# Last and first weight pieces by tile of rows, kept norms as two row operations, and new lane scripts in a whole-model fp32 kernel

## The reference

```
for i in range(4):
    x = x + 0.5 * swiglu(rmsnorm(x, ffn1_norm[i]), ffn1_w_gu[i], ffn1_w_down[i])
    h = rmsnorm(x, mix_norm[i])
    m = (gated_deltanet, stick_breaking, dsa_sparse, gated_deltanet)[i](h, ...)
    x = x + m
    x = x + 0.5 * swiglu(rmsnorm(x, ffn2_norm[i]), ffn2_w_gu[i], ffn2_w_down[i])
x = rmsnorm(x, final_norm)
for l in range(2):
    mix = mixer_sublayer(x, ...)      # GLA, gMLP and MoBA branches, gated, then w_out
    x = layer_norm(ALPHA * x + mix, ln1_g[l], ln1_b[l])
    ff = square(relu(x @ w_ff1[l])) @ w_ff2[l]
    x = layer_norm(ALPHA * x + ff, ln2_g[l], ln2_b[l])
```

## Time and profile before

| | |
|---|---|
| median of 3 runs | 3136.65 us (3131.71 to 3138.2) |
| the profiled execution: its time / its span | 3133.97 / 3132.2 us |
| busy: TensorE, VectorE, ScalarE, GpSimd | 2981.8, 1785.0, 1608.3, 138.6 us |
| mean DMA rate over the span | 164 GB/s |
| stages: a feed-forward stage (905 to 1096) | 191.0 us, TensorE busy 191.0 |
| gdn (208 to 396), mixer2 (2180 to 2455), dsa (1285 to 1393) | 188, 275, 108 us, TensorE busy 170.4, 257.5, 87.8 |

### The profile page before, as it was taken

One profiled execution on the slowest core, in us unless ns is written; L12 is line 12 of the kernel. 1 busy time (PEld: TensorE's weight loads), 2 busy tenths in 40 slices (PEclk: granted clock), 3 DMA queues, 4 the chain that ended last, 5 costly groups with the idle time before them and its releaser, 6 DMA issues.

```text
span 3132.2 us, 36486 instructions
## 1 busy us (share of the span) xinstructions
PE 2981.8 (95%) x15042; PEld 2523.4 (81%) x15042; DVE 1785.0 (57%) x2147; ACT 1608.3 (51%) x2048; POOL 138.6 (4%) x122
## 2 busy tenths in 40 slices
PE   8999899999999999989999998998999998999998
PEld 6888788888988888768888887887878787878786
DVE  5558455455565455565555585654655645655644
ACT  5447754444454354555444467644556553456552
POOL 0004200000000000000000033000000000000000
PEclk9999999999999999989999999999999999999999
DMA  6554155555545565425555541455545555545553
GB/s 220 179 181 141 43 162 188 179 184 182 167 148 184 179 188 181 167 81 184 186 181 188 169 138 65 148 183 178 168 139 177 167 183 179 161 135 179 170 177 132
DMA packets 372694, 512.12 MB, mean 164 GB/s; under 512 B 11409, under 2 KB 239889, under 8 KB 372529
## 3 DMA queue, kind: packets, MB, share of 16 engines
q1 hardware_dynamic: 372528, 509.80, 51.3%
HBM read 508.70 MB, written 1.05 MB: 163 GB/s over the span
## 4 chain that ended last, share of the span: by engine, by line
PE 82%; DVE 6%; ACT 6%; DMA 2%; issue 1%; POOL 1%; SPq 0%; POOLq 0%; DVEq 0%; ACTq 0%
PE ps L424 24%; PE ps L426 24%; PE ps L425 24%; PE ps L509 3%; PE ps L496 2%; DVE lo L549 2%; ACT hi L531 2%; PE ps L456 1%; DVE qkv L1365 1%; PE ps L457 1%; PE ps L458 1%; PE ps L480 1%; POOL junkp L1557 1%; DMA raw<-in_ffn_w_gu 1%; POOL goz L1560 0%
## 5 line engine op out<-in xcount | busy, mean ns | idle before, releaser
L549 DVE TENSOR_TENSOR lo<-raw,hi 128x2048 fp32r<-128x2048 f32 (+1 forms) x479 | 1072.3, 2244 | 929.9 <-ACT hi L531 929.4
L531 ACT ACTIVATE hi<-raw 128x2048 fp32r<-128x2048 f32 (+2 forms) x489 | 911.7, 1869 | 706.4 <-DMA raw<-in_ffn_w_gu 254.9
L424 PE MATMUL ps<-hi,xh 128*128 128x512 f32 (+1 forms) x2208 | 876.1, 397 | 8.7 <-DVE xl L624 4.1
L426 PE MATMUL ps<-hi,xl 128*128 128x512 f32 (+1 forms) x2208 | 861.4, 390 | 0.0
L425 PE MATMUL ps<-lo,xh 128*128 128x512 f32 (+1 forms) x2208 | 860.1, 390 | 0.0
L424 PEld LDWEIGHTS ps<-hi,xh 128*128 128x128 f32 x2208 | 416.5, 189 | 92.5 <-issue 6.8
L426 PEld LDWEIGHTS ps<-hi,xl 128*128 128x128 f32 x2208 | 415.8, 188 | 87.6
L425 PEld LDWEIGHTS ps<-lo,xh 128*128 128x128 f32 x2208 | 416.9, 189 | 81.0
L424 PE MATMUL ps<-hi,hh 128*128 128x512 f32 x704 | 276.1, 392 | 0.0
L426 PE MATMUL ps<-hi,hl 128*128 128x512 f32 x704 | 274.2, 390 | 0.0
L425 PE MATMUL ps<-lo,hh 128*128 128x512 f32 x704 | 274.0, 389 | 0.0
(11 more groups left out here) (438 smaller groups left out, 3254.6 us busy)
## 6 DMA issues: line engine op xcount, KB each, us to landing
raw<-in_ffn_w_gu SPq DMA_DIRECT2D x352, 512.0 KB, 4.8
raw<-in_ffn_w_down SPq DMA_DIRECT2D x80, 1024.0 KB, 5.1
raw<-in_w_ff SPq DMA_DIRECT2D x64, 1024.0 KB, 5.4
raw<-in_w_in SPq DMA_DIRECT2D x60, 1024.0 KB, 5.3
raw<-in_gdn_w_in SPq DMA_DIRECT2D x32, 1024.0 KB, 5.7
raw<-in_sb_w_in SPq DMA_DIRECT2D x12, 1024.0 KB, 5.2
raw<-in_w_branch SPq DMA_DIRECT2D x12, 1024.0 KB, 5.0
raw<-in_ffn_w_down SPq DMA_DIRECT2D x16, 512.0 KB, 3.5
```

Of the source, the lines that this page charges most:

```text
L424: e.matmul(o, a1, r1, start=kk == 0, stop=False)
L426: i = e.matmul(o, a2, r1, start=False, stop=kk == kts - 1)
L531: k.e.activation(k.m.hi[q % RING][:, 0:n], k.m.raw[q % RING][:, 0:n], ACT.Copy).then_inc(*k.up("act_piece_hi", ("hi", q)))
L549: k.e.tensor_tensor(m.lo[i][:, 0:n], m.raw[i][:, 0:n], m.hi[i][:, 0:n].bitcast(F32), ALU.subtract).then_inc(*k.up("dve_piece_lo", ("split" ...
```

## The change

In parts:

1. **Late pieces.** The last piece of a stage (`late` 1), or the last three where a kept norm follows (`late` 3), is run for tile 0 first and then for tile 1 (`tensor_piece` with `ts`; `tensor_out`). `vector_out` takes its residuals in that order.
2. **First pieces.** mixer2 starts with `mu` and `mz`, ff2 with its first two column groups, the first three pieces of which are run for tile 0 and then for tile 1 (`tensor_rows_two`); the stages that start with columns (gdn now with `k` instead of `ba`; sb) run the first halves of their first two pieces, then the second halves (`first=2`).
3. **Kept norms.** The statistics come from bn_stats for the rms norm too (mean and variance, then mean² + variance); each tile has its own root. x becomes (x - mean) * gain, then x * root + bias, both scalar_tensor_tensor over 128x512 (for the rms norm x * root * gain alone). x is turned per tile (`tensor_turn_kept`), `xh` and `xl` are plain copies and differences. `rows_gained` is gone, on GpSimd too. The norm is now a lane in the script, with `next` in all stages.
4. **Output** in two transfers, one a tile.
5. **Scripts** written out for all stages, gdn's new. Gelu, Silu and Sin of mixer2 have a step of their own, `gelu`. Some waits are added that the new orders need.

```diff
 class Plan:
     def out(self, W, kts):
         for s in range(2):
             self.rows(("dn", self.g, s), W, 512 * s, 512, kts)
+        self.late |= set(range(len(self.pieces) - self.lates[self.g], len(self.pieces)))
     def gdn(self, t, name, i):
+        self.cols(("k", g), W, 1024, 4)
         self.cols(("ba", g), W, 3984, 1)
-        self.cols(("k", g), W, 1024, 8)
+        self.cols(("k", g), W, 1024, 8, first=4)
...
+        self.late.add(self.of[("dn", g, 1)][-1][0])
     def mixer2(self, t, name, l):
+        for n, c0 in (("mu", 2064), ("mz", 2576)):
+            self.rows((n, g), W, c0, 512, 8)
...
     def steps(self, p):
-        if len(dims) == 2 and dims[0] == 8:
+        if len(dims) == 2 and dims[0] == 8 or p in self.late:
             return 2
...
+        self.late = 3 if after else 1
...
+def tensor_rows_two(k, plan, pids, xh, xl, ready):
+    banks = {pid: tensor_banks(k, pid, 512) for pid in pids}
+    pieces = [(pid, piece) for pid in pids for piece in plan.of[pid]]
+    for t in range(2):
+        for pid, piece in pieces[:3]:
+            yield from tensor_piece(k, plan, pid, piece, (t,), banks[pid], xh, xl, 8, 512, ready)
+    pid, piece = pieces[3]
+    yield from tensor_piece(k, plan, pid, piece, (0, 1), banks[pid], xh, xl, 8, 512, ready)
...
+def tensor_out(k, plan, si, h, l, kts, ready):
+    banks, pieces = {}, [(("dn", si.g, s), piece) for s in range(2) for piece in plan.of["dn", si.g, s]]
+    early = len(pieces) - si.late
+    for pid, piece in pieces[:early]:
...
+        yield from tensor_piece(k, plan, pid, piece, (0, 1), banks[pid], h, l, kts, 512, ready)
+    for t in range(2):
+        for pid, piece in pieces[early:]:
...
+            yield from tensor_piece(k, plan, pid, piece, (t,), banks[pid], h, l, kts, 512, ready)
+def tensor_turn_kept(k, g, t):
+    for s in range(2):
+        b = k.take("xT", g, t, s)
         k.wait_ge(*b.before)
+        k.wait_ge("x", g, t, s)
+        for j in range(4):
+            i = k.e.transpose(b.ps[:, j * P:(j + 1) * P], k.m.x[:, t, (4 * s + j) * P:(4 * s + j + 1) * P], k.m.C(C_ID))
...
 def vector_norm(k, si):
+    for t in range(2):
+        mean, var, rt = (st[:, c:c + 1] for c in (88 + 2 * t, 89 + 2 * t, 94 + t))
...
+        e.bn_aggr(st[:, 88 + 2 * t:90 + 2 * t], st[:, 64 + 12 * t:76 + 12 * t]).then_inc(*k.up("dve_bn", ("ms" if ln else "var", g, t)))
...
         if ln:
+            k.wait_ge("ms", g, t)
+            for s, (xs, gain, _) in enumerate(x):
+                e.scalar_tensor_tensor(xs, xs, mean, gain, ALU.subtract, ALU.mult).then_inc(*k.up("dve_x_normed", ("xc", g, t, s)))
+            k.wait_ge("rt", g, t)
+            for s, (xs, _, bias) in enumerate(x):
+                k.wait_ge("xc", g, t, s)
+                e.scalar_tensor_tensor(xs, xs, rt, bias, ALU.mult, ALU.add).then_inc(*k.up("dve_x_normed", ("x", g, t, s)))
...
+FFN_SCRIPT = """
+W x1 W W W gate W W W W W turn W gate W W gate gate W W W W turn W W W W W gate W W W W turn W W W gate W turn
+W gate W turn turn W gate turn gate W W W W W W W W W turn W W W turn W gate W gate W W W W W turn turn W out
+W W W W W W W W W W W W W next out out W W
+"""
...
 GDN_SCRIPT = """
+clear x1 rbc W c3 W c0 rbc W E ba W E W W gates gates E W gates W E c2 gates W W W nk gates gates W c2 c0 E W
+nk nk W c1 nk E nk kT c0 c2 W nk c0 c2 c1 c3 E W c1 c3 W c1 E W inv c3 E kT W E W W inv gates W W W W W W c0 W
+c3 c2 E c1 c0 W c2 E c0 nq W Z W c2 W nq nq c2 c0 W nq nq nq c0 c2 qk c1 c2 c3 sv c1 c3 W Z c0 c1 rows rows c1
+c0 c3 rows c1 c3 rows c2 c0 gate c1 c3 a0 qk c1 c2 a0 a0 a1 a0 c3 a0 qk qk a1 c3 a0 a0 a1 W a1 a1 a1 W W a1 W
+W out W W next out W out
 """
...
+SB_SCRIPT = """
+x1 W rbc W E W W W E rbc E W E W W W E W W heads W heads W heads W E heads W E heads E W heads W heads W W v W
...
+DSA_SCRIPT = """
+W x1 W W W p0 W normq normq W W W normq W p1 normk W normk W W normk normk W W qi index_q normk W uq turn_q
+index_q index turn_q W index index index uv index index index turn_q turn_q W index index W uk W turn_k
+attention attention attention attention attention attention attention attention attention W W attention
+attention attention out W W W W next out out W W
...
+MIXER2_SCRIPT = """
+W W x1 W mu W W angles mz W lr clear W angles W W W W W decays W W decays W decays gk decays W gq W decays W W
+decays decays gv gla W decays W W decays W W gla W gla W gg gla gla gla gelu gla gla gla W W W W gmlp gla gla
+gla gmlp gmlp gla gmlp gmlp gla gla moba gla oq W W ok gmlp W W gmlp W gla W gmlp W W moba ov gmlp gmlp moba W
...
+next out W norm W
+"""
...
     for r in range(2):
         for s in range(2):
-            k.wait_ge("xr", infos[-1].g, r, s)
-    e.dma_start(out[0].rearrange("(t p) d -> p t d", p=P), m.x[:, :, :]).then_inc(*k.up("dma_out", ("out",), by=16))
+            k.wait_ge("x", infos[-1].g, r, s)
+        e.dma_start(out[0, r * P:(r + 1) * P, :], m.x[:, r, :]).then_inc(*k.up("dma_out", ("out", r), by=16))
```

More of the change, by code:

```diff
@@ L241, in run, with __init__ @@
         assert name not in script or next(lane, "end") == "end", name
-def to_next(si):
-    return ["next"] if si.after is None and not si.last else []
 class Plan:
-    def __init__(self, t, stages):
-        self.pieces, self.of, self.stage, self.pool = [], {}, [], set()
+    def __init__(self, t, stages, lates):
+        self.pieces, self.of, self.stage, self.pool, self.late, self.lates = [], {}, [], set(), set(), lates
         for g, (name, *arg) in enumerate(stages):
@@ L403, in tensor_rows @@
     w = n // half
[L404 to L433, removed]
@@ L434, in tensor_rows @@
+    for t in ts:
         if k0 + cnt == kts:
-            for b in banks[0] + banks[1]:
+            for b in banks[t]:
                 k.close(b)
-        yield
[L440 to L446, removed]
-        k.wait_ge(*b.before)
[L448 to L461, removed]
-                k.close(b)
-            yield
@@ new lines, in tensor_rows_two, with tensor_cols @@
+def tensor_rows_two(k, plan, pids, xh, xl, ready):
[6 more added lines that the diff above has]
+    yield from tensor_piece(k, plan, pid, piece, (0, 1), banks[pid], xh, xl, 8, 512, ready)
+def tensor_cols(k, plan, pid, xh, xl, ready, first=0):
+    pieces = plan.of[pid]
+    steps = [tensor_col_piece(k, plan, pid, piece, xh, xl, ready) for piece in pieces]
+    for _ in range(2):
+        for step in steps[:first]:
+            next(step)
+            yield
+    for step in steps[first:]:
+        for _ in range(2):
+            next(step)
+            yield
@@ L945, in turn @@
             yield
[L947 to L948 removed]
+    run(script, {"W": vector_pieces(k, plan, g), "x1": vector_x1(k, si), "turn": turn(),
+                 "out": vector_out(k, si, 1.0, keep=ALPHA), "norm": vector_norm(k, si), "next": vector_next(k, nxt)})
 def gdn_room(m):
@@ L2690, in tensor_program @@
         TENSOR[si.name](k, plan, si, nxt, SCRIPT[si.name](plan, si))
-        if si.after and not si.last:
-            run(["x0"], {"x0": tensor_turn_x(k, nxt.g, 0)})
 def scalar_program(k, plan, infos):
@@ L2700, in scalar_program @@
         SCALAR[si.name](k, plan, si, nxt, SCRIPT[si.name](plan, si))
-        run(["norm"], {"norm": scalar_norm(k, si)})
-        if si.after and not si.last:
-            run(["x0"], {"x0": scalar_turned_x(k, nxt, 0)})
 def vector_program(k, plan, infos):
@@ L2711, in vector_program @@
         VECTOR[si.name](k, plan, si, nxt, SCRIPT[si.name](plan, si))
-        run(["norm"], {"norm": vector_norm(k, si)})
-        if si.after and not si.last:
-            run(["x0"], {"x0": vector_turned_x(k, nxt, 0)})
-        elif si.after:
-            vector_gained(k, nxt, 0)
-            vector_gained(k, nxt, 1)
 def pool_program(k, plan, infos):
-    for si, nxt in zip(infos, infos[1:] + [None]):
-        if si.before:
-            run(["rows", "rows"], {"rows": (step for s in range(2) for step in pool_gained(k, si, s))})
+    for si, nxt in zip(infos, infos[1:]):
         if si.name in POOL:
```

462 lines of the change are left out of this document (251 added, 211 removed).

## The result

The changed kernel takes **3034.68 us** (median of 4 runs, 3033.87 to 3036.35) where the kernel before took 3135.72 beside it (4 runs): ratio 0.968, 95% interval 0.9663 to 0.9696, 101 us faster.

A forecast was written before the change was run, and what follows sets the result against it. TensorE, busy 2981.8 of 3132.2 us, bounds the kernel; only its idle time and lower-clock stretches can be won. Terms 31 + 6 + 8 + 16 + 16 + 5 - 6 = 76 us gave 3061 us, range 3022 to 3108.

The forecast's parts named there:

- mixer2: Inner gap before the sum of gv's matmuls goes, no VectorE split before the sum, four W steps ahead: gain 16 us.
- gdn: Wait behind the convolution in both gdn stages falls from 11 to some 3 us: gain 16 us, or 0 if splits collide.
- likeliest case: The forecast's main case, all terms summed to 76 us gained: chance 0.59, own range 3040 to 3082 us.
- slower: Rival: feed-forward gates ahead of splits make 17 places cost about 5 us each, 3146 us; chance 0.09.
- Kept norms with late pieces: Four boundaries before and after mixer2 and ff2 lose 14 us instead of 44.7: gain 31 us, 22 to 35.
- The end: Behind the last matmul: 9.4 us from tile 1's end, 4.4 of it for the output to land; gain 6 us.
- Ordinary boundaries: Last piece by tiles shortens stage entries: two gdn entries 2.0 us each, sb 4; together 8 us.
- inner gaps stay: Rival: gaps inside gdn, mixer2 and dsa remain as chains keep their length, 3098 us; chance 0.17.
- dsa: Top-k mask steps come before three weight steps and two pieces run inside attention: gain 5 us, 0 to 10.
- Feed-forward scripts: Some 17 places in eight stages where the gate makes ScalarE and the next split wait: loss of 6 us.
- More is won: Rival: inner gaps go whole, lanes lose nothing, TensorE's busy time holds lower-clock work; 110 us gained, 3027; chance 0.11.

The follow-up runs named there:

- both_whole: Changed kernel with only the last piece by tiles at kept norms, turning of tile 0 behind the last matmuls, and mixer2's and ff2's first pieces for both tiles: 3075.19 us.
- late_one: Changed kernel with only the last weight piece, not three, tile by tile at the four kept norms, turning of tile 0 behind the last matmuls: 3058.63 us.
- parts: Changed kernel: second gdn without GpSimd splits, both mixer2 with two W steps ahead, second also a split ahead of the sum, output in one transfer: 3053.78 us.
- old_lanes: Changed kernel with the old interleaving in feed-forward stages, sb, dsa and gdn, and gdn's old piece order; tails, kept norms and mixer2 as changed: 3064.64 us.
- pool_sets: Changed kernel with one of gdn's five GpSimd splits given back to VectorE, the first in the first gdn, the second in the second: 3039.17 us.
- improved: Changed kernel with the norm's early table load behind the last Silu of the last feed-forward stage, and tile 0's turning one step later at three kept boundaries: 3028.33 us.

## Why the prediction was right or wrong

The direction and the mechanism of the kept norms and of mixer2 were right; gdn, of equal size in the forecast, failed. The sum was 25 us short (76 for 101): six terms gave more than forecast, together some 40 us, and gdn gave 16 less. So that the total fell into the range is in part luck, and it missed the likeliest case, 3040 to 3082. Two sums don't come out as written. The ends of the terms taken half together give 3049 to 3089 for that case; and the rival "slower" subtracts the 6 us of the gates from the gain and then counts its places in full, so its 3146 should be 3140.

- *Kept norms with late pieces*, 31 (22 to 35), measured 39 by both_whole. The waits came as the prediction had them: 8.5 in all where it had 2.5 a boundary, 1.4 to 1.9 at three of them and 3.4 at the first, for the table load that the working did not have. The step that was mis-sized is the lower clock: the 1.0 a boundary that I added for it was not paid in the changed kernel's trace, and what the old pauses cost does not end with the windows of the earlier trace rows. late_one measures such a price: 11 us more of waiting cost 21. That the gain is overlap and not the cheaper norm is shown by both_whole, for the four inner boundaries.
- *The end*, 6, measured 7.7. The chain of passes is as laid out (4.9 us from the last matmul's start to the issue); the transfer is the part mis-sized, 3.1 us for a last half where I took 4.4 for the whole. 1.4 of it is shown by the single transfer in parts.
- *Ordinary boundaries*, 8. gdn's entries gave 2.3 each for 2.0. sb gave 8.1 for 4: 4.3 of that with its interleaving, which the term had not counted, so the entry's share is 3.8. The sizes were right. Of the two reasons given for gdn, old_lanes shows that the split's place in VectorE's queue is needed; the last piece by tiles does nothing without it.
- *gdn*, 16 (0 to 22), measured near 0: the two stages are 4.2 us shorter, and their entries give 4.5. This is the step that failed, by the rival "inner gaps stay", which the page "SBUF — State Buffer" of the Trainium skill (section "SBUF: two separate sides") had spoken for with its exclusive lock; the trace agrees with it. A GpSimd split of 6.73 beside two of VectorE that take 8.88, and a second one with a convolution of 5.6 us under it, are the old collision at other steps (the convolution that held TensorE up before now takes 2.5); two waits at the head of the stage (1.4 and 2.7) are new. The waits of 0.4 us and more inside the first gdn add up to 16.0 us before and 16.5 after, and TensorE's work at the lower clock in the two gdn stages grew from 11.8 to 18.0 us. But the lock is half of it: without any GpSimd split the stage gets longer, since VectorE's queue then has a split ahead of the chain's copy.
- *mixer2*, 16 (4 to 18). With the kept norms it makes the last four stages and the ffn2 ahead of them 60.8 us shorter, for 31 + 16; 39 taken off, 22 are left for it. The trace of the kernel before holds as much inside mixer2: the two waits of 7.3, 8.3 us of work at the lower clock behind them (half of it lost), and smaller waits of 0.7 and 1.1 in each layer, 22.4 in all. The gap went as the step says, and having it back costs 13.0 in one layer, 5 more than the waits themselves. Of the two reasons given the first holds (no split of VectorE ahead of the sum), the second doesn't: two W steps instead of four cost 0.2.
- *dsa*, 5 (0 to 10), measured 13. Mis-sized: the wait for the mask fell from 8.9 to 1.8 where I held the keys' turning against it, and two stretches at the lower clock in the old attention (PEclk 0.83 over 21 us in old_lanes, 1.00 now) went with it. Cover inside attention is 4 of it; the rest has no run of its own.
- *Feed-forward scripts*, a loss of 6, measured a gain of 5, 3.5 of it by the interleaving. Some 2.9 lie at the entries of the three later ffn1 stages, where the waits of the first 8 us fell from 1.2 to 1.6 us each to 0.44; the prediction had given these entries nothing. The gates do stand ahead of splits: ScalarE's longest wait at one grew from 3.8 to 9.7 us, and VectorE's total wait for hi fell from 929 to 588 us. But nothing that TensorE needs behind them is late: it is busy for 190.6 us of the 191.0 us window, and the rest is the one wait of 0.44 at an entry. So the rival "slower" falls; its places cost nothing.

"More is won" was right in its sign, that TensorE's busy time held work at the lower clock. Its 3027 was nearly met, but by other terms than its own: its 22 for gdn did not come.

## What to carry to other kernels

When a bound engine pauses, price the pause at its length plus what the clock does behind it: here 11 us of longer waits cost 21, while waits of 1.3 to 2.1 us mostly cost only themselves, and once 1.6 us more. To take a norm off the path, give the bound engine the other tile's matmuls over it; at the four inner boundaries the cheaper norm gave next to nothing without that, and it paid only at the end of the kernel, 6 of 7.7 us. And look for what stands ahead of the awaited operation in the in-order queue: moving one split past a sum was worth 13 us, and taking a contended helper's work back won 3.7 us in one kernel and lost 3.7 in the other, by where the work landed in VectorE's queue.

## What the runs showed of the hardware

- In these traces the granted clock fell to 0.5 behind all the waits of 3.4 to 9.7 us, unless it was there already, and at the head of gdn behind waits of 1.36 and 2.65 with 3.3 us of work between them. Behind shorter waits it varied. Behind the 1.9 us in dsa and the 2.1 at the first boundary it stayed at 1.00 in the changed kernel and fell for 3.4 us in pool_sets (in dsa in improved too). Inside the changed kernel's second gdn it fell behind a wait of 1.89, for 10.2 us. At gdn's entry of the kernel before, a wait of 3.1 let it fall in one execution and not in another.
- A broadcast copy of GpSimd took 4.8 us beside two splits of VectorE that took their usual 4.5 together, and 0.57 alone; a split of GpSimd between two of VectorE stretched the pair to 8.9. One by one: the VectorE split that ran first kept its 2.28, the GpSimd split beside it took 6.73 instead of 4.55, and the next VectorE split 6.68 instead of 2.28. The one that started second was held up each time. Where the GpSimd split started first (at 1864.86 of the changed kernel), it kept its 4.53, and one operation of the convolution took 3.56 instead of 0.4; a copy out of PSUM under the next such split (at 1876.25) kept its 0.69.
